# Final transposes in the weights' bank, an earlier weight split, no table preload, and a reordered gate tail in a hybrid transformer pair

## The reference

```python
def reference(x, ...):
    x = first_block(x, ...)      # x += hybrid_mixer(rms_norm(x)); x += hierarchical_moe(rms_norm(x))
    return second_block(x, ...)

def hybrid_mixer(h, ...):
    proj = h @ w_in
    mqk, mv, mo, mi, mf, aq, ak, av = jnp.split(proj, IN_SPLITS, axis=-1)
    qk = jax.nn.silu(causal_conv(mqk, conv_w, conv_b))
    hm = mlstm_chunkwise(mq, mk, mv, mi + b_igate, mf + b_fgate)       # 4 heads of 128
    hm = rms_norm(jax.nn.sigmoid(mo) * hm, m_norm_w)
    ha = diff_attention(aq, ak, av, ...)                               # 4 heads, two softmaxes each
    return jnp.concatenate([hm, ha], axis=-1) @ w_out

def second_block(x, p, ...):
    # pooling mixer and sliding-window attention, layer norm, squared-relu feed-forward, layer norm
    gate = jax.nn.sigmoid(h @ w_ple_gate[i] + b_ple_gate[i])
    return h + gate * (p[i] @ w_ple[i])
```

## Time and profile before

| | us |
|---|---|
| three runs | 1451.41, 1454.59, 1458.12 |
| median | 1454.59 |
| the profiled execution | 1451.41 |
| its span, first to last instruction | 1449.1 |
| TensorE busy | 1401.7 (97%) |
| VectorE busy | 964.2 (67%) |
| ScalarE busy | 773.5 (53%) |
| GpSimd busy | 194.8 (13%) |
| granted TensorE clock, mean | 0.987 of full |

### The profile page before, as it was taken

One profiled execution on the slowest core, in us unless ns is written; L12 is line 12 of the kernel. 1 busy time (PEld: TensorE's weight loads), 2 busy tenths in 40 slices (PEclk: granted clock), 3 DMA queues, 4 the chain that ended last, 5 costly groups with the idle time before them and its releaser, 6 DMA issues.

```text
span 1449.1 us, 20106 instructions
## 1 busy us (share of the span) xinstructions
PE 1401.7 (97%) x6753; PEld 1070.4 (74%) x6754; DVE 964.2 (67%) x1169; ACT 773.5 (53%) x963; POOL 194.8 (13%) x233
## 2 busy tenths in 40 slices
PE   6999999999899999999999999999899999999998
PEld 6887677555677777777776777666788888888886
DVE  6854543445999999999899987674854224343185
ACT  5433444124699999999898983453144212342131
POOL 2021001010322222222121210061000000000000
PEclk8999999999999999999999999999999999999999
DMA  9131125215899999999999977012313133124131
GB/s 349 59 117 59 58 76 191 102 57 205 312 396 410 413 412 413 415 412 404 413 411 403 409 299 260 1 59 87 113 62 116 63 112 117 62 113 160 60 115 58
DMA packets 60965, 302.55 MB, mean 209 GB/s; under 512 B 9700, under 2 KB 11810, under 8 KB 48108
## 3 DMA queue, kind: packets, MB, share of 16 engines
q1 hardware_dynamic: 49420, 282.15, 49.6%
q10 hardware_dynamic: 6288, 11.44, 2.2%
q0 software_dynamic: 5200, 8.18, 1.7%
HBM read 291.74 MB, written 18.87 MB: 214 GB/s over the span
## 4 chain that ended last, share of the span: by engine, by line
PE 75%; DMA 4%; DVE 4%; issue 2%; ACT 2%; POOL 0%; DVEq 0%; ACTq 0%; SPq 0%; POOLq 0%
PE ps L744 13%; PE ps L1025 12%; PE ps L1010 11%; PE ps L783 7%; PE ps L776 4%; DMA ring<-in_w_gate 4%; PE ps L594 4%; PE ps L845 3%; PE ps L753 3%; PE ps L1059 3%; PE ps L524 2%; PE ps L917 2%; PE ps L475 2%; PE ps L733 1%; PE ps L628 1%
## 5 line engine op out<-in xcount | busy, mean ns | idle before, releaser
L2120 DVE TENSOR_TENSOR ring_r<-ring,hi 128x2048 fp32r<-128x2048 f32 (+1 forms) x224 | 431.3, 1981 | 19.0 <-ACT hi L1560 16.9
L1560 ACT ACTIVATE hi<-ring 128x2048 fp32r<-128x2048 f32 (+1 forms) x224 | 362.9, 1662 | 9.4 <-DMA ring<-in_w_gate 7.5
L2132 DVE TENSOR_TENSOR ring_r<-ring,ring_two 128x2048 fp32r<-128x2048 f32 (+1 forms) x46 | 102.2, 2259 | 112.7 <-ACT ring_two L1578 112.6
L1578 ACT ACTIVATE ring_two<-ring 128x2048 fp32r<-128x2048 f32 (+1 forms) x46 | 83.9, 1868 | 128.6 <-PE ps L1025 121.5
L744 PE MATMUL ps<-ring_r,XTS 128*128 128x512 f32 x512 | 128.7, 394 | 2.6 <-DVE XTS L2125 1.8
L1229 POOL TENSOR_TENSOR rsv<-msv,half 128x1 f32<-128x1 f32 (+2 forms) x32 | 33.2, 1039 | 711.5 <-DVE msv L1746 693.1
L1025 PE MATMUL ps<-ring_two,ats 128*128 128x512 f32 x512 | 126.6, 389 | 0.0
L744 PE MATMUL ps<-hi,XTS 128*128 128x512 f32 x512 | 126.5, 389 | 0.0
L783 PE MATMUL ps<-hi,HIDS 128*64 128x512 f32 x512 | 123.0, 392 | 0.0
L524 PE MATMUL ps<-ring_r,ring_r 128*128 128x512 f32 x448 | 115.1, 406 | 1.3 <-ACT ring_r L1382 0.7
L744 PEld LDWEIGHTS ps<-ring_r,XTS 128*128 128x128 f32 x512 | 97.1, 190 | 25.6 <-issue 3.2
(11 more groups left out here) (350 smaller groups left out, 2166.8 us busy)
## 6 DMA issues: line engine op xcount, KB each, us to landing
ring<-in_w_up SPq DMA_DIRECT2D x32, 2048.0 KB, 18.0
ring<-in_w_gate SPq DMA_DIRECT2D x32, 2048.0 KB, 16.1
ring<-in_w_down SPq DMA_DIRECT2D x32, 2048.0 KB, 16.5
ring<-in_w_ff SPq DMA_DIRECT2D x16, 2048.0 KB, 8.1
ring<-in_w_in SPq DMA_DIRECT2D x9, 2048.0 KB, 9.2
ring<-in_w_out SPq DMA_DIRECT2D x4, 2048.0 KB, 9.4
results<-M SPq DMA_DIRECT2D x4, 1024.0 KB, 17.3
ring<-results SPq DMA_DIRECT2D x8, 512.0 KB, 6.8
```

The source lines that it names most:

```text
L1560: act.activation(HI[u][:, c], ring[:, s, c], ACT.Copy).then_inc(w_hi, 1)
L1578: act.activation(hi_of(u, a, part_size(u)), raw_of(u, a, part_size(u)), ACT.Copy).then_inc(w2_hi, 1)
L2120: vec.tensor_tensor(ring_r[s][:, c], ring[:, s, c], HI[u][:, c].bitcast(F32), ALU.subtract).then_inc(w_lo, 1)
L2132: vec.tensor_tensor(raw_of(u, a, n, ring_r), raw_of(u, a, n), hi_of(u, a, n).bitcast(F32), ALU.subtract).then_inc(w2_lo, 1)
```

## The change

Five edits: the eight final transposes go into `AT_BANK` (bank 6) instead of `O_BANKS` (7 or 1); one more PLE product stands ahead of the rank and one less behind it; the preload of the Exp table is gone; the two parts of the split of "mv" are made in steps 0 and 1 on ScalarE (2 and 4 before) and their remainders in steps 2 and 3 on VectorE (3 and 5 before); in the last loop VectorE adds the bias of tile n + 1 ahead of its wait for sigmoid n instead of behind the two operations on tile n.

```diff
             def final_d(i):
                 left(pe, ("O", i, "d"))
-                transposes(("F", i, "d"), O_BANKS[i % 2], ND, HEADS)
+                transposes(("F", i, "d"), AT_BANK, ND, HEADS)
 
             def final_m(i):
                 pe.wait_ge(fin_ready, i + 1)
-                transposes(("F", i, "m"), O_BANKS[i % 2], NM, HEADS)
+                transposes(("F", i, "m"), AT_BANK, NM, HEADS)
...
-            for n in range(3):
+            for n in range(4):
                 extra(n)
 
             pe.wait_ge(oh_ready, 1)
...
-            for n in range(3, 6):
+            for n in range(4, 6):
                 extra(n)
...
-            act.preload_act_table(ACT.Exp)
             act.wait_ge(zeroed, 16 * TT)
...
+                if n in (0, 1):
+                    hi_1(5, n)
                 if n in (8, 9):
                     hi_1(6, n - 8)
                 if n % 2 and n // 2 < len(FILL_1):
                     filled_out(n // 2)
-                if n in (2, 4):
-                    hi_1(5, n // 2 - 1)
...
-                if n in (3, 5):
-                    lo_1(5, n // 2 - 1)
+                if n in (2, 3):
+                    lo_1(5, n - 2)
...
+                if n + 1 < 2 * TT:
+                    gate_in_(n + 1)
                 vec.wait_ge(gate_act, n + 1)
                 if t == 0:
                     vec.wait_ge(ple_back[c], 16)
                 step(vec.tensor_tensor(OUT2[:, c, t, :], GT[:, n % 2, :], OUT2[:, c, t, :], ALU.mult))
                 vec.tensor_tensor(OUT2[:, c, t, :], OUT2[:, c, t, :], X[:, t, s], ALU.add).then_inc(out_ready, 1)
-                if n + 1 < 2 * TT:
-                    gate_in_(n + 1)
```

## The result

| | before | after |
|---|---|---|
| median, first measurement | 1453.89 us (4 runs) | 1470.97 us (4 runs) |
| second measurement | 1454.36 (23) | 1470.69 (6) |
| profiled execution, its span | 1451.41, 1449.1 | 1469.85, 1467.5 |
| granted TensorE clock in it | 0.987 | 0.983 |

The change makes the kernel slower: the ratio is 1.0111, interval [1.0081, 1.0143], and 1.0122 [1.0098, 1.0146] in the second measurement. That is some 16 us where 9.2 were forecast; the time lies above the range.

The account below looks back on a forecast made before the run. TensorE was taken to bound the kernel, without idle time in attention and as a chain in the expert stage. Terms 4.6 + 2.2 + 1.7 + 0.7 = 9.2 us on 1454.6 gave 1463.8, 0.63% slower, range 1457 to 1470.

Parts of the forecast that it names:

- What bounds the kernel: Attention stage: TensorE never idle, so its waits are paid in full; expert stage: a delay ahead moves it whole.
- rival of the late loads: Expert stage: the shifted start makes loads land faster, saving 7.2 us, total 1456.6; chance 0.11.
- that of the hidden hand-overs: Attention: copies out of bank 6 come before the transposes ask, saving 5.5 us, total 1458.3; chance 0.10.
- Final transposes in bank 6: Attention: TensorE waits for copies at seven places, 5.5 us, less 0.9 given back at the last transpose: +4.6 us.
- forecast's first six delays: Attention items 7, 11, 15, 19, 23, 27: TensorE's waits for bank 6 copies, 0.59, 1.04, 1.47, 0.51, 0.62, 0.73 us.
- Exp table and the earlier split: Attention start: the third filler's matmuls wait on ScalarE, splits 1.8 us and table load 0.4: +2.2 us.
- One extra product: Ahead of the rank: four more passes delay the rank and all behind it by 1.7 us, nothing gained behind.
- The tail: Output stage's end: VectorE has two tiles left after TensorE's last one, +0.7 us, bounds 0 and 1.4.
- the clock: Wait near 131 in attention lowers TensorE's clock: 1.8 us lost, perhaps twice that, 1465.6 up to 1467.5; chance 0.14.
- the forecast's case: Whole kernel: the four terms hold, median 1463.8 us, spanning 1460.5 to 1467; chance 0.58.

Follow-up runs that it names:

- the bank run: Only the final transposes moved to bank 6, against the kernel before: 1464.04 us against 1456.18, ratio 1.0068 [1.0043, 1.0093].

## Why the prediction was wrong

**What bounds the kernel** held: every wait added to TensorE in the attention stage reached the end, and the expert stage kept its length to within 0.8 us. The rival of the late loads never came (to landing 8.2 us at the start and 20.1 from 660 us on, the growth of the earlier trace rows); that of the hidden hand-overs neither, for all seven are in the trace.

**Final transposes in bank 6**: predicted +4.6, measured +5.7. The forecast's first six delays are met as idle times: 0.59, 1.04, 1.47, 0.51, 0.62, 0.73 against 0.60, 1.06, 1.49, 0.47, 0.61, 0.74 in the bank run (the seventh, put at 0.50 because part of it was waited for before, is 0.88). But in the whole change the steps came 0.78, 1.24, 1.72, 0.68, 0.80, 0.94 and 0.59 later, 6.75 in all, some 0.2 more each for the first six: eight transposes in one run took 1.04, two runs of four, with the wait between them, 0.60 and 0.63. That is the part of the term that was left out. What the last one gives back is 1.07 for 0.9.

**Exp table and the earlier split**: predicted +2.2 = 1.8 + 0.4, measured 2.19, and 1.80 for the split alone. Right. The load shows its 1.28 and the exponential 1.29 behind its start. The 1.38 us of drain that the Trainium skill ("ScalarE: Activation LUTs", "What ACT_TABLE_LOAD costs") has behind a load are not in this trace.

**One extra product**: the rank 1.7 us later as predicted; 0.3 of it was taken back in the waits behind (the first gate product 1.4 later). **The tail**: 0.5 for 0.7, the high side of what a measurement can't see.

**The step that failed is the clock.** It stood as a rival at 0.14, with one fall of 1.8 us and perhaps 3.6, and the forecast's own sum priced it at nothing, because the gap of 0.94 at 317 left the clock alone. (TensorE had two more gaps in that stage, 0.59 and 0.91 us at 172 to 178, behind which the clock stayed at 1.00 too.) The one fall that it did price, 1.8 us, measured 1.3 to 1.6 in the twelve products behind the wait. What the prediction had wrong is that such a wait has its fall every time, not at odds of 0.14, and that the shorter waits can have one too. The fall behind filler 2 is certain: all 6 profiles with that wait empty have it, and none of the 11 without the wait, nor of the 3 with products in it. Beside it the mean clock is lower by 0.0034 with the bank edit alone, some 3.7 us; with six executions that is uncertain by 1.6 us. A fall follows two of the 28 hand-over waits at once, at 191 and 284 us above, and none the other 26. In all the clock is 4 to 6 us of the 16: 4.6 by the slope (uncertain by 0.8), 4.1 by filling the waits (by 1.4), 6 if the 9.8 of the edits' own waits are taken from the mean of 15.8. The Trainium skill, "TensorE: Matmul & The Clock Gate", section "A second HAM failure mode: psum-queue depth-cycling", says that frequent short idle times between groups of matmuls, as PSUM banks are cycled, make the clock go back and forth. The bank run's mean clock of 0.9818 for 0.9852 agrees in its direction. Why the same short wait has a fall behind it in one execution and none in the next, and where the other falls of the whole change come from, no run here settles.

With the structure at its measured 10.2 for 9.2 and the clock at 4.6, the sum would have been 1469.4. The stated spread of the forecast's case, 1460.5 to 1467, is not half a microsecond for each of its four terms, which is 1461.8 to 1465.8; either would have been too low. Of the 8 us of falls in the first pair of profiles, some are chance: that pair set a lucky execution of one (1451.4 of a median near 1455.7) beside a usual one of the other. The 3.1 in the second block need not all be, for the fall near 1070 us is in all three profiles of the new kernel, and near 1060 in one of three of the kernel before.

## What to carry to other kernels

Where TensorE runs without a gap, price each new wait as its length plus a fall of the clock, here 1.3 to 1.6 us behind a wait of 1.8 to 2.2, and smaller waits as their length plus an uncertain share, here 2 to 5 us beside the 5.7 of the seven hand-overs. Before one profile is compared with another, compare the granted clock and count its falls; two executions of one program differed by 8 us. Products put into a wait hold the clock up there, but that is a repair of the wait's second cost, and the wait itself stays.

## What was not expected of the hardware

The scatter of this kernel, 1450 to 1463 us over the runs, goes mostly with the granted clock: 1.11 us for each 0.001 of its mean. A short wait is followed by a fall in one execution and by none in the next. In the profile of the kernel before that took 1458.66 us, one came behind the wait of 0.67 us at 694 us, where that of 1450.44 us waited 0.58 us and had none. And falls come also where TensorE has no wait: with only the last final transpose moved it had no gap in the 10 us before, and at 328 us, behind the router's small products, the clock fell to 0.57 in a window of 4 us. The same instructions took 1.07 and 3.60 us in the first profile of the kernel before:

```profile
328.18 1.73 PE L475 MATMUL ps<-ident,M 128*128 128x128 f32 x8
329.70 4.67 PE L594 MATMUL ps<-ring,HT 128*128 128x512 f32 x8
```

And a higher mean clock isn't time by itself: with products in three waits of the kernel before it rose from 0.9852 to 0.9876 over 12 executions, and the time stayed.
